# Forgetting-attention weighted sums: value high and low parts in one 128-column stationary block, two matmuls in place of three

## The reference, cut to what matters

```
s = einsum('bqhd,bkhd->bhqk', qb, k) * scale
s = s + cqb[..., :, None] - c_bhs[..., None, :]
s = where(causal, s, -inf)
p = softmax(s)
out = einsum('bhqk,bkhd->bqhd', p, v)
```

## Time and profile before

| what | value |
|---|---|
| median of 3 runs | 1298.28 us (1297.55 to 1298.31) |
| span of the profiled execution | 1296.9 us |
| median less the span (what lies around it) | 1.4 us |
| busy share PE, weight load, DVE, ACT, POOL | 99%, 85%, 70%, 47%, 36% |
| fox stage, 784 to 900 us: PE, DVE, ACT, POOL busy | 115.4, 72.0, 75.1, 37.8 of 116 us |
| granted TensorE clock, mean | 0.999 |

### The profile page before, as it was taken

The page is one execution under the profiler, slowest core; times in us unless marked ns, Lnnn a source line. Parts: engine busy times, 40 slices in busy tenths (PEclk is TensorE's granted clock), DMA queues, the critical chain, the costliest instruction groups (busy, mean ns, idle before and its releaser), DMA issues.

```text
span 1296.9 us, 18193 instructions
## 1 busy us (share of the span) xinstructions
PE 1287.1 (99%) x7006; PEld 1097.8 (85%) x7006; DVE 909.7 (70%) x1266; ACT 605.3 (47%) x999; POOL 467.2 (36%) x208
## 2 busy tenths in 40 slices
PE   9999999999999999999999999999999999999998
PEld 7887888898778888888889788898879999998886
DVE  7999826899292466656498674567989999985442
ACT  5223323435343466656654445578464444443223
POOL 2444544455444442452555343323430000015441
PEclk9999999999999999999999999999999999999999
DMA  4333423224723422326143345443323333323331
GB/s 164 98 98 106 121 91 98 72 91 116 290 81 98 135 59 83 82 62 216 49 146 114 115 149 146 133 113 114 98 65 131 98 99 119 110 84 112 114 97 66
DMA packets 47875, 143.66 MB, mean 111 GB/s; under 512 B 6032, under 2 KB 6032, under 8 KB 47024
## 3 DMA queue, kind: packets, MB, share of 16 engines
q1 hardware_dynamic: 43984, 129.88, 32.7%
q10 hardware_dynamic: 3808, 12.64, 2.7%
HBM read 121.46 MB, written 10.49 MB: 102 GB/s over the span
## 4 chain that ended last, share of the span: by engine, by line
PE 74%; issue 13%; POOL 7%; DVE 2%; ACT 1%; DMA 1%; SPq 0%; POOLq 0%; ACTq 0%
PE bank L2101 23%; PE bank L2103 23%; PE bank L2102 23%; POOL w_lo L701 7%; PE bank L2334 2%; PE bank L2323 1%; PE bank L2324 1%; DMA raw<-stream 1%; DMA x<-x_in 1%; PE bank L2125 0%; PE bank L2479 0%; PE bank L2480 0%; DVE zv L1834 0%; PE bank L2653 0%; ACT f_prob_t L993 0%
## 5 line engine op out<-in xcount | busy, mean ns | idle before, releaser
L701 POOL TENSOR_TENSOR w_lo<-raw,w_hi 128x1024 fp32r<-128x1024 f32 (+1 forms) x146 | 372.8, 2558 | 524.8 <-ACT w_hi L769 524.7
L769 ACT ACTIVATE w_hi<-raw 128x1024 fp32r<-128x1024 f32 x149 | 156.0, 1053 | 167.6 <-PE bank L2103 87.9
L746 POOL TENSOR_TENSOR w_lo<-raw,w_hi 128x1024 fp32r<-128x1024 f32 x22 | 53.6, 2441 | 263.0 <-DVE w_lo L1958 204.5
L2101 PE MATMUL bank<-pool_xg,w_hi 128*128 128x512 f32 x248 | 98.6, 398 | 0.2 <-POOL w_lo L701 0.2
L2102 PE MATMUL bank<-pool_xg,w_hi 128*128 128x512 f32 x248 | 98.1, 396 | 0.0
L2103 PE MATMUL bank<-pool_xg,w_lo 128*128 128x512 f32 x248 | 98.1, 396 | 0.0
L2101 PE MATMUL bank<-right,w_hi 128*128 128x256 f32 x336 | 94.4, 281 | 0.0
L2103 PE MATMUL bank<-right,w_lo 128*128 128x256 f32 x336 | 94.1, 280 | 0.0
L2102 PE MATMUL bank<-right,w_hi 128*128 128x256 f32 x336 | 94.1, 280 | 0.0
L2040 DVE TENSOR_TENSOR act<-acts,act 128x512 fp32r<-128x512 f32 x22 | 47.6, 2166 | 51.1 <-ACT act L1222 51.1
L2101 PE MATMUL bank<-y_hi,w_hi 128*128 128x512 f32 (+1 forms) x216 | 81.0, 375 | 0.0
(11 more groups left out here) (449 smaller groups left out, 3722.9 us busy)
## 6 DMA issues: line engine op xcount, KB each, us to landing
raw<-stream SPq DMA_DIRECT2D x187, 512.0 KB, 3.6
raw_x<-stream SPq DMA_DIRECT2D x18, 512.0 KB, 4.9
spill<-x ACTq DMA_DIRECT2D x2, 2048.0 KB, 7.8
xg_spill<-mla_xg ACTq DMA_DIRECT2D x2, 2048.0 KB, 12.0
rope_q<-turned_hl SPq DMA_DIRECT2D x64, 64.0 KB, 2.5
zx<-xg_spill SPq DMA_DIRECT2D x2, 1536.0 KB, 9.5
stacked<-fq SPq DMA_DIRECT2D x24, 128.0 KB
stacked<-fk SPq DMA_DIRECT2D x24, 128.0 KB
```

The source lines that it names most:

```text
L701: pool.tensor_tensor(w_lo[:, j % RING, 0:width], raw[:, j % RAW, 0:width], plain(w_hi[:, j % RING, 0:width]), ALU.subtract).then_inc(tile_ ...
L746: pool.tensor_tensor(w_lo[:, s, 0:D], raw[:, d % RAW, 0:D], plain(w_hi[:, s, 0:D]), ALU.subtract).then_inc(tile_lo, 1)
L769: act.activation(w_hi[:, t % RING, 0:width], raw[:, t % RAW, 0:width], ACT.Copy).then_inc(tile_hi, 1)
L2101: pe.matmul(target, a_hi, b_hi, start=start, stop=False)
```

## The change

Values are stored per head as a block of 128 columns: the 64 high parts and beside them the 64 low parts. One matmul with this block gives high by probability in rows 0 to 63 of bank 5 and low by probability in rows 64 to 127, and so two matmuls a block, one with the probabilities' high part and one with their low part, hold all four products (low by low is new). The two halves of the bank are added on the way out: ACT copies rows 64 to 127 into a new buffer `low_half`, and DVE adds rows 0 to 63 and `low_half` where it copied before. ACT's square root for the layer norm moves from after head 3 to after head 4.

```diff
-        fv_hi, fv_lo = (place(48 + 8 * i, f"fv_{i}", [P, NB, D_ATTN], f32r) for i in range(2))
+        fv = place(48, "fv", [P, NB, FOX_HEADS, 2, FOX_D], f32r)
+        low_half = place(155, "low_half", [FOX_D, S])
...
-                act.activation(fv_hi[:, b, :], bank[V_BANK[b]][:], ACT.Copy, scale=inv_t[:, b:b + 1]).then_inc(fv_hi_done, 1)
+                act.activation(fv[:, b, :, 0, :], by_head(bank[V_BANK[b]][:]), ACT.Copy, scale=inv_t[:, b:b + 1]).then_inc(fv_hi_done, 1)
...
+            def copy_low_half(h):
+
+                act.wait_ge(fox.weighted, h + 1)
+                if h:
+                    act.wait_ge(fox.out, h)
+                act.activation(low_half[:], bank[5][FOX_D:P, :], ACT.Copy).then_inc(low_half_copied, 1)
...
             for h in range(FOX_HEADS):
+                if h:
+                    copy_low_half(h - 1)
                 transposed_high(fox, h, f_prob_t_hi, (0, 1))
...
-                if h == 3:
+                if h == 4:
                     act.wait_ge(ln_prepared, 1)
                     act.activation(rstd[:], rstd[:], ACT.Sqrt).then_inc(ln_rstd, 1)
...
             for pair in range(FOX_PAIRS - 1):
                 attn_square(pair)
+            copy_low_half(FOX_HEADS - 1)
             attn_high(FOX_PAIRS - 1)
...
-                dve.scalar_tensor_tensor(fv_lo[:, b, :], bank[V_BANK[b]][:], inv_t[:, b:b + 1], plain(fv_hi[:, b, :]),
+                dve.scalar_tensor_tensor(fv[:, b, :, 1, :], by_head(bank[V_BANK[b]][:]), inv_t[:, b:b + 1], plain(fv[:, b, :, 0, :]),
                                          ALU.mult, ALU.subtract).then_inc(fv_lo_done, 1)
...
                 rows = slice(FOX_D * (h % 2), FOX_D * (h % 2 + 1))
-                dve.tensor_copy(attn[rows, h // 2, :], bank[5][rows, :]).then_inc(fox.out, 1)
+                dve.wait_ge(low_half_copied, h + 1)
+                dve.tensor_tensor(attn[rows, h // 2, :], bank[5][0:FOX_D, :], low_half[:], ALU.add).then_inc(fox.out, 1)
...
-                a = slice(P * (h // 2), P * (h // 2 + 1))
                 for b in blocks:
                     pe.wait_ge(fox.prob_t_lo, NB * h + b + 1)
                     r = slice(COLUMN[b], COLUMN[b + 1])
-                    last = three(bank[5][:, P * b:S], fv_hi[:, b, a], fv_lo[:, b, a], f_prob_t_hi[:, r], f_prob_t_lo[:, r],
-                                 b == 0, b == NB - 1)
+                    v = fv[:, b, h, :, :].rearrange("p a d -> p (a d)")
+                    pe.matmul(bank[5][:, P * b:S], v, f_prob_t_hi[:, r], start=b == 0, stop=False)
+                    last = pe.matmul(bank[5][:, P * b:S], v, f_prob_t_lo[:, r], start=False, stop=b == NB - 1)
```

More of the change, by code:

```diff
@@ L450, in build @@
         v_summed, fv_hi_done, fv_lo_done = sem("v_summed"), sem("fv_hi_done"), sem("fv_lo_done")
+        low_half_copied = sem("low_half_copied")
         gate_abs_ready, gate_log, log_f_ready = sem("gate_abs_ready"), sem("gate_log"), sem("log_f_ready")
@@ L565, in both, with by_head @@
             return ap.unsqueeze(1).to_broadcast([P, 2, ap.shape[-1]])
+        def by_head(ap):
+            return ap.rearrange("p (h d) -> p h d", h=FOX_HEADS)
         def halves(ap):
```

## The result

The changed kernel took 1299.83 us (median; 1298.42 to 1302.29), the kernel before 1298.28 (1297.3 to 1300.28) beside it on the same chip, 20 executions of each. The ratio is 1.0013 with a 95% interval of 1.0007 to 1.0019: about 1.5 us slower, which is within 0.2%. The forecast was 1299.6. Thirty-two matmuls went, and the kernel became a little slower.

A forecast was written before the change was run, and what follows sets the result against it. PE was taken to set the pace up to head 4, ACT and DVE to limit each head's close from head 5. Gaining 5.0 us and giving back 6.3 made 1298.28 + 1.3 = 1299.6 us; range 1296.2 to 1302.9.

The forecast's parts named there:

- Heads 0 to 4, the gain of 2.5 us: Copies and additions fit into waits; PE gains 0.63 us a head, so head 4's transposes come 2.5 us early.
- The rival that the cover holds: ACT's late heads have more room than read, so PE keeps all 5.0 us: 1293.3; chance 0.16, wholly or mostly.
- The prices: Per head: ACT copy 0.60 us, DVE addition 0.66; root 0.20 and table loads 1.40 each, moved one head later.
- The rearranged store, set at nothing: Storing the values as high and low parts costs nothing: same four instructions on each engine, covered by PE's work.
- the rival that it is held up beside POOL: DVE's addition takes 1.65 us more at heads 4 and 5, beside POOL: 3.3 us worse, 1302.9; chance 0.06.
- Head 5: Load, root and copy precede L993's successor, at 869.87; transposes (2, 3) at 871.3; PE waits 2.85 us.
- Head 6: Exps at 873.7, L993's successor 1.3 us late at 881.8, transposes (2, 3) at 883.3; PE waits 2.2 us.
- The clock as a rival: Clock falls behind PE's long waits in heads 5 and 6: 1302.6 for 3 us of it, 1310 for all; chance 0.06.
- a granted clock under 1: Listed sign that the forecast is wrong: PE's granted clock dropping below full speed.
- Head 7: Reciprocal of 886.45 comes 1.3 us late; 0.63 each of heads 6 and 7 is lost to waits; mean 1.3 late.
- 1 us either way: Bound for how DVE's layer-norm and `attn_low` instructions fall beside POOL's.
- The sum: Over eight heads: 5.0 us gained, 2.85, 2.2, 0.63 and 0.63 given back, together 6.3: 1.3 us slower.

The follow-up runs named there:

- M alone: Kernel before with only two matmuls a block for three (M): no ACT copies or additions, root after head 3, values' low product left out; 1295.69 us.
- R alone: Kernel before with only the square root moved from after head 3 to after head 4 (R); 1300.88 us, ratio 1.0019.
- the room alone: Control: kernel before with only the layer-norm centrings and shifts on DVE spread over more heads; 1297.08 us, ratio 0.9996.
- M and C: Changed kernel with the square root back after head 3, keeping two matmuls, ACT copies and additions (C); 1297.65 us, ratio 0.9994.
- M and R: Changed kernel without ACT's copies and the additions, root still after head 4, values' low product left out; 1297.81 us, ratio 0.9997.
- C and R: Changed kernel with a third matmul a block put back, repeating the first; 1302.54 us, ratio 1.0037.
- the fill ahead: Changed kernel with PE's first fill of head 5 (24 matmuls) moved ahead of transposes (2, 3); 1300.38 us, ratio 1.0019.
- the copies moved forward: Changed kernel with the root back after head 3 and three of ACT's low-half copies issued earlier; 1296.41 us, ratio 0.9985.

## Why the prediction was right

**Heads 0 to 4, the gain of 2.5 us.** Right. Head 4's L998 starts at 857.24 in place of 859.77, 2.53 us earlier, four times 0.63. Head 5's first transposes are 3.18 us early (five times 0.63 is 3.15). The rival that the cover holds is out by the two waits of PE, and by M alone, which does not keep 5.0 either.

**The prices.** The copy takes 0.60 as taken from L993. Two copies on the path were to cost 1.2 us and the additions nothing: the traces of the ledger say 1.25 and 1.36 for both, the medians about 2. The root and its loads cost 2.5 by their place. The rearranged store, set at nothing, is nothing: four instructions of 0.69 us on ACT and of 0.75 on DVE in both traces. The addition takes 0.68, in all eight heads (0.683 to 0.685), where POOL is at work and where it is not: the rival that it is held up beside POOL is out. The copy that it replaces took the same 0.68.

**Head 5.** L998 at 869.90 (said 869.87), L1692 at 870.59 (870.5), transposes (2, 3) at 871.41 (871.3) with a wait of 2.90 (2.85). The load is counted rightly at about 1.40, and R alone shows the price of the place: 2.5 us for two loads of 1.28 and a root. The Trainium skill (ScalarE: Activation LUTs, "What ACT_TABLE_LOAD costs") adds a drain of about 1.38 us for each load. The rows disagree once more: the load at 872.65 ends at 873.93 and the exp starts at 873.95.

**Head 6.** Here the terms of the sum were too small by some tenths and one was missing. The exps start at 873.95 (said 873.7), L998 at 882.22 (881.8), L1692 at 883.01 (882.4) and the transposes at 883.85 (883.3). PE's wait was said to be 2.2 and was 1.34. What made the difference is the clock: the 24 matmuls from 871.91 to 876.18 took 4.27 us, and took 2.93 before, so PE came 1.3 us later to a place where it would else have waited those 1.3 us longer (the last section has what the traces show for that).

**The clock as a rival.** The text named "a granted clock under 1" as a sign of being wrong and priced the rival at 3 us or more. The clock did fall, so half of that reasoning failed: its price. It had counted every slower microsecond of PE as lost, in a head whose end is set by ACT and DVE. On the path lay only the transposes themselves, 0.85 us instead of 0.70, and behind them ACT's second pair of L998 some 0.2 us later. The Trainium skill (TensorE: Matmul & The Clock Gate, "What's actually happening") has the lower level come back with idle time of PE; the trace agrees behind the wait of 2.90 us.

**Head 7.** The reciprocal starts at 887.78, 1.33 after 886.45 (said 1.3), the first transposes 1.34 later than before, and so does the mean. This term is right partly by luck: L1692 of head 6 was 1.86 late, not 1.3. About 0.5 came back at `attn_low`, which took 0.81 us at 886.63 and took 1.60 at 884.93 before. In both traces POOL splits a weight tile there, in the changed kernel until 886.89 and before until 885.97, so that before the two ran beside each other for longer (the timeline of DVE before):

```profile
884.93 1.60 DVE L1791 SCALAR_TENSOR_TENSOR attn<-attn,cols 128x512 fp32r<-128x512 f32 x1
```

That this is the cause was not tried; the prediction had put 1 us either way on it.

**The sum.** 1.3 us slower was said of the span, and 1.3 it was. Its parts are shared out otherwise than forecast: 2.85, 2.2, 0.63 and 0.63 were to be given back, 6.3 together; PE's waits beyond those of before come to 4.8 us (2.90, 1.34, and 0.6 in small ones from head 7 on) and the slower matmuls to 1.3. The medians differ by 1.5. The step from span to median was taken as 1.4 us, but every execution on record lies 1.66 to 1.85 us over its own span; so the profiled execution of before was itself some 0.3 us above its median, and the 0.2 between 1.3 and 1.5 is of that size.

## What to carry to other kernels

An engine that is busy for 99% of a kernel can still be worth nothing to relieve: read in the stage itself which engine arrives last at the point where a loop closes, and whether it has idle time there, before a saved instruction is counted in full. Of 5.0 us of matmuls 2.7 arrived with nothing added on ACT and DVE, in a kernel that leaves a product out. The whole change kept 3.2 once its added work and the layer norm's stood in heads where ACT and DVE had room. A square root with its two table loads cost 2.5 us merely by standing one head later. Save on the busy engine and make room on its helpers in the same step: the room alone brought 0.6 us, which the medians cannot tell from nothing.

## What the runs showed that was not expected

The granted clock fell behind waits of PE of 1.40, 2.10, 2.27, 2.90 and 4.27 us (M and C; M and R; C and R; the change; the fill ahead), and stayed up behind 1.35 and 1.47 us (the copies moved forward; R alone). The length of the one wait does not order these cases, 1.40 against 1.47. Nor does the kernel alone settle it: of the eleven executions of R alone, two have a mean granted clock of 0.997 and five one of 1.000, and of the eleven of M and C nine have 0.998 and one has 1.000. The 74 executions of the kernel before that were timed beside these runs have 0.998 to 1.000. What decides was not found out.

At the lower level the 256-column matmuls of the mix start 0.213 us apart, 0.12 at the upper, and in the changed kernel they keep that distance from 872.3 to 874.8 us, in M and C from 870.8 to 873.8. What the fall cost is best read from the traces of the ledger. The kernel before, M alone and R alone have no fall in the stage, and there M gives 2.59 us; from R (no fall) to M and R (fall) M gives 2.53, so the fall took less than 0.1. R costs 2.46 between two traces without a fall, and 2.52 from M (none) to M and R (fall). In these traces ACT and DVE set the end of the next head, and what PE lost on the way there went into a wait.

The executions without a trace do not settle it. In R alone the two at 0.997 took 1300.22 and 1300.89 us and the five at 1.000 had 1300.94 in the middle, so nothing was lost; in M and C the one at 1.000 took 1297.65, the median of them all. But three of the 74 of before, at 0.998, took 1300.41 to 1300.88 us, and two of M and R, at 0.997, took 1300.65 and 1300.72, about 2.5 and 3 us over their medians. Where in these the clock fell, and whether it fell because of the lost time or made it, no trace shows.
